# The m gates of the second half: a second turn by seven products, with moved row sums and other PSUM banks

## The chip, the cores and the metric

One core of one Trainium2 chip. The metric is the device time of one execution in microseconds (us), the median of several runs. The kernel before takes 2076.13 us (three runs, 2075.77 to 2076.33).

## The reference, cut to what matters

The kernel computes two blocks of a language model for 256 tokens of width 2048: a gated MLP mixer and then a block with attention, an mLSTM, a gated merge, an output projection and a feed-forward part. The change lies in the gated merge of the second block:

```python
g_a = jax.nn.sigmoid(z[..., OFF_GA:OFF_GM])
g_m = jax.nn.sigmoid(z[..., OFF_GM:D_IN])        # z = h @ w_in, h is 256 x 2048
merged = (g_a * jnp.einsum('bse,ed->bsd', a_out, w_proj_a[l])
          + g_m * jnp.einsum('bse,ed->bsd', m_out, w_proj_m[l]))
x = x + jnp.einsum('bsd,de->bse', merged, w_out[l])
```

The m gates are the product of h with 2048 columns of w_in. `gm0` computes their first 1024 columns, `gm1` the second 1024.

## The kernel before

**Number format.** Every matrix is split into a high and a low part, `w_hi` and `w_lo`, and a product is three matmuls (high by high, high by low, low by high). A weight chunk is 128 partitions by 1024: two blocks of 128 rows by 512 columns. It comes by DMA (SyncE's queue) into the four-slot ring `raw`; ScalarE copies it to `w_hi` (`high_of_chunk`, L1279), VectorE subtracts to get `w_lo` (`low_of_chunk`, L1778), TensorE uses both. `w_hi` and `w_lo` have four slots too: ScalarE's copy for item n waits until TensorE has ended item n - 4. In the loops over items, the turn for item n prepares item n + 4.

**Items.** The order of the work is written out by hand in `ITEMS`; every engine walks through it in its own loop. A phase such as gm0 covers two output tiles of 256 tokens by 512 columns (the halves, four PSUM banks of `g`, one for each half and token tile) and runs over 2048 rows of weights in four turns of 512 rows. A turn is done in one of two ways. *Plain*: four items C0 to C3, each a chunk of 12 matmuls. *By seven products* (Winograd's form of Strassen's scheme on 2 x 2 blocks): items named by their product, 1 to 7, each of 6 matmuls, 42 in place of 48. The seven products need sums of row blocks of the activations (`sums_hi`, `sums_lo`, made once for each turn and used again by the second half of the phase pair) and sums of weight blocks (`block_sums`, L1792: VectorE adds in place into the blocks that SyncE loaded, after the w_lo of products 1, 5 and 6 and of the item behind product 1). Products 1, 5, 6, 7 gather in banks of their own in `xs`, across all turns that go by products; products 2, 3, 4 go straight into `g`. After the last product 6, ScalarE copies product 1 out (`first_product`), VectorE combines the four (`own_products`, `last_of_own_products`), and `gate_m_result` (L2328) adds or subtracts them from the halves of `g`.

**How a seven is mixed with plain items.** While a product takes half of a plain item's matmuls, it needs a whole w_hi copy and a whole w_lo subtraction. So a seven is interleaved with the four items of a plain turn: `MIXED` is 1, C0, 5, 7, C1, 6, 3, C2, 4, 2, C3, and `MIXED_LATE` (used in gm1 and out2) is C0, 1, C1, 5, 7, C2, 6, 3, C3, 4, 2. gm0 runs turns 3 and 2 by products, mixed with plain turns 0 and 1. gm1 runs plain turn 0, then turn 3 by products mixed with plain turn 1, then plain turn 2.

**What lies around gm1.** The phases follow as gm0, pa0, pm0, gm1, pa1, pm1, out2; pa and pm are the projections of the two branches, 8 plain items each. At pm0's end VectorE makes the merged quarters: `merged_low(0)`, then `m_projected(0, 1)` (L2347 the gate product, L2349 the addition, which releases `merged_ready`). TensorE transposes the second quarter behind gm1's item 1 (`merged_turned(1)`, eight transposes into banks 0 and 1 of `xs`); ScalarE takes it with `merged_high(1)` in loop turn 1, VectorE with `merged_low(1)` (L2325, called at L2361) in loop turn 2, behind the w_lo and the block sum of that turn, and raises `merged_lo_ready` to 2. gm1's product 1 waits for that (L1197), since it writes bank 0. The merged values `g_hi` and `g_lo` take the memory of gm's row sums of turn 2, which is why gm1 before could use those of turn 3 alone.

Of the kernel before, what the change touches and what calls it, by code (L numbers as in the profile page):

```python
# [5 lines left out]
P = 128  # L6
# [52 lines left out]
for _name, _w in (("a_norm", KD), ("norm1", KD), ("norm2", KD), ("b_s", GROUPS),  # L59
# [33 lines left out]
    "down": (((3, None), (4, None), (8, None), (9, None), (5, 0), (6, 1), (7, 2), (10, None)),  # L93
             ((3, 0), (7, None), (4, 1), (5, 2), (8, 6), (9, None), (10, None))),
    "gm0": (((0, 3), (1, 2)),),
    "gm1": (((0, None), (1, 3), (2, None)),),
    "out2": (((0, None), (2, 1), (3, None)),) * 2,
}

# [50 lines left out]
for _name, _counts in PHASES:  # L150
    FIRST_ITEM[_name] = len(ITEMS)
    if _name == "ug":
        for _g in range(GROUPS):
            for _step in UG_ORDER if _g else UG_FIRST:
                if isinstance(_step, int):
                    ITEMS.append(Item("ug", _g, _step, UG_TURN, None, None))
                else:
                    _turn, _k = _step[0], int(_step[1][1])
                    ITEMS.append(Item("ug", _g, 0, _turn, _k // 2, 2 * _turn + _k % 2))
        continue  # L160
    if _name in MID_ORDER:
        for _g, _order in enumerate(MID_ORDER[_name]):
            for _step in _order:
                if isinstance(_step, int):
                    ITEMS.append(Item(_name, _g, _step, MID_TURN, None, None))
                else:
                    _turn, _k = _step[0], int(_step[1][1])
                    ITEMS.append(Item(_name, _g, 0, _turn, _k // 2, 2 * _turn + _k % 2))
        continue
    if _name not in WIDE_STEPS:  # L170
        ITEMS += [Item(_name, None, 0, None, None, _k) for _k in range(sum(_counts))]
        continue
    for _g, _steps in enumerate(WIDE_STEPS[_name]):
        for _turn, _by_products in _steps:
            for _what in (PLAIN if _by_products is None else MIXED_LATE if _name in ("gm1", "out2") else MIXED):
                if _what in PLAIN:
                    _k = int(_what[1])
                    ITEMS.append(Item(_name, _g, 0, _turn, _k // 2, 2 * _turn + _k % 2))
                else:
                    ITEMS.append(Item(_name, _g, _what, _by_products, None, None))  # L180
# [5 lines left out]
def in_ring(item):  # L186
# [39 lines left out]
             FIRST_ITEM["down"] + 13: ("down", B22), FIRST_ITEM["down"] + 14: ("down", B21),  # L226
             FIRST_ITEM["gm0"] - 4: ("gm0", B11), FIRST_ITEM["gm0"] - 3: ("gm0", B12),
             FIRST_ITEM["gm0"] - 2: ("gm0", B22), FIRST_ITEM["gm0"] - 1: ("gm0", B21),
             FIRST_ITEM["gm1"] - 2: ("gm1", B11), FIRST_ITEM["gm1"] - 1: ("gm1", B12),
             FIRST_ITEM["gm1"]: ("gm1", B22), FIRST_ITEM["gm1"] + 2: ("gm1", B21),  # L230
             FIRST_ITEM["out2"] - 2: ("out2", B11), FIRST_ITEM["out2"] - 1: ("out2", B12),
             FIRST_ITEM["out2"]: ("out2", B22), FIRST_ITEM["out2"] + 2: ("out2", B21)}

# [61 lines left out]

def own_banks(phase, g):

    if phase in ("ug", "vv"):
        return UG_OWN_BANK
    if phase == "side":  # L300
        return {0: TWO_BANKS, 1: FIRST_APART, 2: FIRST_APART}.get(g, ONE_BANK)
    return OWN_BANK
# [92 lines left out]
def build(nc, x, x_tokens, stream, w_s, params, gain_rows, final_rows, gate_w, identity, consts, out):  # L395
# [48 lines left out]
    class Mid:  # L444
# [3 lines left out]
        def __init__(self, sb, name, blocks, halves, sums):  # L448
# [2 lines left out]
            self.half = [sb(f"{name}_half{h}", "y", at * kib, [P, 2, COLS]) for h, at in enumerate(halves)]  # L451
            (self.p1, self.p7), (self.u_a, self.p5) = ((of[:, 0, :], of[:, 1, :]) for of in self.half)

    class Gated:


# [53 lines left out]
    for name, phase, groups, blocks, halves in (  # L510
# [43 lines left out]
    gm_wide = Wide(sb, "gm", [("mix", 0), ("mix", 4 * kib), ("y", 72 * kib), ("y", 76 * kib)],  # L554
                   [("y", 88 * kib), ("y", 64 * kib)], [("y", 92 * kib), ("y", 80 * kib)], ("y", 68 * kib),
                   ("y", 84 * kib), ("y", 32 * kib))
    out2_wide = Wide(sb, "o2", [("mix", 0), ("mix", 4 * kib), ("y", 48 * kib), ("y", 52 * kib)],
                     [("y", 56 * kib)], [("y", 60 * kib)], ("y", 72 * kib), ("y", 76 * kib), ("y", 0))
    g_hi = sb("g_hi", "y", 64 * kib, [P, KD, S], F32R)
# [13 lines left out]
    out1_wide = Wide(sb, "o", [("mix", 0), ("mix", 4 * kib), ("x", 12 * kib), ("x", 4 * kib)],  # L573
                     [("h", 8 * kib), ("h", 12 * kib)], [("h", 24 * kib), ("h", 28 * kib)], ("h", 0), ("h", 16 * kib),
                     ("y", 88 * kib))
    by_phase = {"vv": mid_sums, "v": v_wide, "out1": out1_wide, "gm0": gm_wide, "gm1": gm_wide, "out2": out2_wide, "down": down_wide}
    u_sum = sb("u_sum", "mix", 4 * kib, [P, 4, S])

    def wide(phase, g):
# [72 lines left out]
    with block:  # L652
# [71 lines left out]
        def _(pe):  # L724
# [149 lines left out]
            def opens_own(item):  # L874

                key = (item.phase, item.group, -item.product)
                new = key not in opened
                if new:
                    opened.add(key)
                    if item.phase in MID_ORDER:  # L880
                        opens_mid(item)
                    elif item.phase == "ug" and item.group and item.product in (1, 5):

                        pe.wait_ge(sem["sv_read"], item.group + 1)
                    elif item.phase == "ug" and item.group:

                        pe.wait_ge(sem["y_lo_ready"], item.group)
                    elif own_ahead(item.phase, item.group):
                        pe.wait_ge(sem["own_read"], own_ahead(item.phase, item.group))
                return new  # L890
# [293 lines left out]
            for p in range(2):  # L1184
                gm, pa, pm = f"gm{p}", f"pa{p}", f"pm{p}"
                for n in range(items_of(gm)):
                    at_item = FIRST_ITEM[gm] + n
                    item = ITEMS[at_item]
                    pe.wait_ge(lo_ready, at_item + 1)
                    if item.product:  # L1190
                        if item.product == 1 and p == 0:

                            pe.wait_ge(sem["m_done"], M_HEADS)
                            pe.wait_ge(sem["sums_lo_ready"], sums_ahead("gm0") + sum_slot("gm0", item.turn) + 1)
                        if item.product == 1 and p == 1:

                            pe.wait_ge(sem["merged_lo_ready"], 2)  # L1197
                        ins = wide_product(item, norm_mid.hi, norm_mid.lo, at_item % RING)
                    else:
                        ins = wide_chunk(item, norm_mid.hi, norm_mid.lo, at_item % RING)  # L1200
                    ins.then_inc(mm_done, 1)
                    if p and n == 1:
                        merged_turned(1)
                for n in range(8):
                    one(pa, n // 4, n % 4, tokens(pa, n // 4, am_hi[:, 0:8, :], am_lo[:, 0:8, :],
                                                  None if n >= 4 or p else "am_lo_ready"))
                for n in range(8):
                    one(pm, n // 4, n % 4, tokens(pm, n // 4, am_hi[:, 8:16, :], am_lo[:, 8:16, :],
                                                  None if n >= 4 or p else "am_lo_ready", 2))
                    if n == 6:  # L1210
                        merged_turned(2 * p)
# [63 lines left out]
        def _(act):  # L1275
# [405 lines left out]
            for p in range(2):  # L1681
                gm, pa, pm = f"gm{p}", f"pa{p}", f"pm{p}"
                for n in range(items_of(gm)):
                    split(gm, n)
                    if p and n == 1:
                        merged_high(1)
                    first_product(gm, FIRST_ITEM[gm] + n)
                for n in range(8):
                    split(pa, n)
                    if n in (1, 3):  # L1690
                        h = n // 2
                        act.wait_ge(group_read[h], group_of(gm, h)[2])
                        by_token(gate_m[h], gate_m[h], ACT.Tanh, scale_half).then_inc(sem["gate_m_ready"], 1)
                for n in range(8):
                    split(pm, n)
                    if n == 6:
                        merged_high(2 * p)
                    if p:
                        sums_high("out2", n - 8)
# [73 lines left out]
        def _(dve):  # L1773
# [119 lines left out]
            def own_products(phase, n):  # L1893
# [3 lines left out]
                for name, g in GROUPS_BY_PRODUCTS:  # L1897
                    if name != phase:
                        continue
                    after = n - product_item(phase, g, last_by_products(phase, g), 6)  # L1900
                    if after == 0:
                        dve.wait_ge(sem["p1_ready"], own_ahead(phase, g) + 1)
                        dve.wait_ge(mm_done, n + 1)
                        link(v.tensor_tensor(u_a[:], p1[:], XS[:, 2, :], ALU.subtract))
                    if after == 2:
                        link(v.tensor_tensor(u_b[:], XS[:, 3, :], u_a[:], ALU.add))
                    if after == 4:
                        link(v.tensor_tensor(u_a[:], XS[:, 1, :], u_a[:], ALU.add))

            def last_of_own_products(phase, n):  # L1910
                u_b, u_d = by_phase[phase].u_b, by_phase[phase].u_d
                for name, g in GROUPS_BY_PRODUCTS:
                    if name == phase and n - product_item(phase, g, last_by_products(phase, g), 6) == 5:
                        link(v.tensor_tensor(u_d[:], XS[:, 1, :], u_b[:], ALU.add))
                        dve.sem_inc(sem["own_read"], 1)

            def v_result(q):
# [433 lines left out]
            for p in range(2):  # L2351
# [14 lines left out]
                        a_projected(p, 0)  # L2366
                for n in range(8):
                    if n == 7:

                        merged_low(2 * p)  # L2370
                        m_projected(p, 1)
                    split(pm, n)
# [243 lines left out]
```

## Time and profile before

| | |
|---|---|
| median of three runs | 2076.13 us |
| the profiled execution | 2076.55 us |
| its span, first to last instruction | 2074.6 us |
| TensorE matmul busy | 2067.9 us (100%) |
| TensorE weight load busy | 1734.9 us (84%) |
| VectorE busy | 1640.2 us (79%) |
| ScalarE busy | 1163.1 us (56%) |
| granted TensorE clock, mean | 1.000 |

In the profile PE is TensorE (PEld its weight loads, which overlap), DVE is VectorE, ACT ScalarE, POOL GpSimd, SP SyncE. L906 is line 906 of the kernel. Matmuls overlap in their pipeline, so the duration of one is longer than the distance to the next. In a timeline row, the brackets behind an instruction tell how long its engine was idle before it and what ended that.

### The profile page before, as it was taken

The numbers are of one execution on the slowest core, as the hardware profiler recorded it, in microseconds if no ns is written. First come the engines' busy times: TensorE is split into PE (matmuls) and PEld (weight loads), VectorE is DVE, ScalarE is ACT, GpSimd is POOL, SyncE is SP. The second block draws the span as 40 slices with busy tenths as digits, with TensorE's granted clock in tenths as the row PEclk, the third lists the DMA queues.
The fourth block names the chain that finished last, engine by engine and source line by source line (L and its number), as shares of the span: only waits on it lengthen the run. The fifth ranks groups of instructions, "written<-read, shape, count | busy, mean of one in ns | idle before, by whom it ended". The sixth has DMA issues, their size and how long they took to land.

```text
span 2074.6 us, 25496 instructions
## 1 busy us (share of the span) xinstructions
PE 2067.9 (100%) x9916; PEld 1734.9 (84%) x9916; DVE 1640.2 (79%) x1846; ACT 1163.1 (56%) x1387; POOL 50.2 (2%) x53
## 2 busy tenths in 40 slices
PE   9999999999999999999999999999999999999999
PEld 7888888888888887878888888888888888888887
DVE  7988788887887876886788668867777777789986
ACT  6666555555556555655555455555555555555553
POOL 0000000000000000110000000000000000000000
PEclk9999999999999999999999999999999999999999
DMA  9667777787684667655475656455655555556663
GB/s 340 205 204 214 224 234 224 213 240 223 247 265 153 217 207 213 208 156 193 134 232 182 204 183 214 159 184 184 193 184 192 193 192 184 193 181 235 222 204 132
DMA packets 117720, 423.30 MB, mean 204 GB/s; under 512 B 13152, under 2 KB 13920, under 8 KB 117344
## 3 DMA queue, kind: packets, MB, share of 16 engines
q1 hardware_dynamic: 109440, 394.66, 57.1%
q0 software_dynamic: 5184, 18.88, 5.3%
q10 hardware_dynamic: 2976, 8.14, 1.1%
q8 instruction: 79, 1.29, 0.2%
q14 instruction: 41, 0.34, 0.1%
HBM read 419.52 MB, written 2.10 MB: 203 GB/s over the span
## 4 chain that ended last, share of the span: by engine, by line
PE 96%; DVE 3%; ACT 1%; DMA 1%; issue 0%; ACTq 0%; DVEq 0%
PE g L906 49%; PE xs L929 9%; PE xs L768 8%; PE g L768 8%; PE g L933 6%; PE g L739 4%; PE xs L774 4%; PE g L774 4%; PE xs L817 1%; DVE w_lo L1785 1%; PE xs L968 1%; PE xs L1101 0%; DMA raw<-in_stream 0%; ACT w_hi L1298 0%; DMA xf<-in_x 0%
## 5 line engine op out<-in xcount | busy, mean ns | idle before, releaser
L1785 DVE TENSOR_TENSOR w_lo<-raw,w_hi 128x1024 fp32r<-128x1024 f32 x631 | 765.2, 1222 | 314.1 <-ACT w_hi L1298 306.5
L1298 ACT ACTIVATE w_hi<-raw 128x1024 fp32r<-128x1024 f32 x631 | 661.8, 1057 | 522.4 <-PE g L906 224.3
L906 PE MATMUL g<-w_hi,in_both 128*128 128x512 f32 x1120 | 356.6, 390 | 1.8 <-DVE w_lo L1860 1.2
L906 PE MATMUL g<-w_hi,mid_both 128*128 128x512 f32 x992 | 320.2, 393 | 0.0
L906 PEld LDWEIGHTS g<-w_hi,in_both 128*128 128x128 f32 x1120 | 210.3, 188 | 47.1 <-DVE w_lo L1785 1.4
L906 PEld LDWEIGHTS g<-w_hi,mid_both 128*128 128x128 f32 x992 | 186.3, 188 | 38.5
L906 PE MATMUL g<-w_lo,in_both 128*128 128x512 f32 x560 | 217.9, 389 | 0.0
L906 PE MATMUL g<-w_lo,mid_both 128*128 128x512 f32 x496 | 193.1, 389 | 0.0
L768 PE MATMUL g<-mlp_both,w_hi 128*128 128x512 f32 x704 | 167.0, 391 | 0.0
L768 PE MATMUL xs<-mlp_both,w_hi 128*128 128x512 f32 x704 | 165.6, 390 | 0.0
L768 PEld LDWEIGHTS xs<-mlp_both,w_hi 128*128 128x128 f32 x704 | 130.7, 188 | 26.2
L768 PEld LDWEIGHTS g<-mlp_both,w_hi 128*128 128x128 f32 x704 | 130.4, 188 | 26.0
L906 PEld LDWEIGHTS g<-w_lo,in_both 128*128 128x128 f32 x560 | 105.2, 188 | 21.4
L906 PEld LDWEIGHTS g<-w_lo,mid_both 128*128 128x128 f32 x496 | 93.2, 188 | 18.7
L906 PE MATMUL g<-w_hi,f_hi 128*128 128x512 f32 x240 | 93.6, 390 | 0.1
L906 PE MATMUL g<-w_hi,f_lo 128*128 128x512 f32 x240 | 93.4, 389 | 0.0
L906 PE MATMUL g<-w_lo,f_hi 128*128 128x512 f32 x240 | 93.4, 389 | 0.0
L774 PEld LDWEIGHTS g<-mlp_both,w_lo 128*128 128x128 f32 x704 | 88.3, 191 | 2.3
L774 PE MATMUL g<-mlp_both,w_lo 128*128 128x256 f32 x704 | 89.0, 283 | 0.0
L774 PEld LDWEIGHTS xs<-mlp_both,w_lo 128*128 128x128 f32 x704 | 87.4, 192 | 1.7
L774 PE MATMUL xs<-mlp_both,w_lo 128*128 128x256 f32 x704 | 87.9, 283 | 0.0
L1298 ACT ACTIVATE w_hi<-d_block 128x1024 fp32r<-128x1024 f32 x49 | 52.0, 1062 | 56.5 <-PE g L906 39.4
(503 smaller groups left out, 3336.8 us busy)
## 6 DMA issues: line engine op xcount, KB each, us to landing
raw<-in_stream SPq DMA_DIRECT2D x631, 512.0 KB, 4.2
d_block<-in_stream SPq DMA_DIRECT2D x28, 512.0 KB, 4.6
o_block<-in_stream SPq DMA_DIRECT2D x24, 512.0 KB, 4.3
v_block<-in_stream SPq DMA_DIRECT2D x20, 512.0 KB, 4.3
ge_block<-in_stream POOLq DMA_DIRECT2D x15, 512.0 KB, 5.5
gm_block<-in_stream SPq DMA_DIRECT2D x12, 512.0 KB, 5.8
ge_block<-in_stream SPq DMA_DIRECT2D x10, 512.0 KB, 4.9
gl_block<-in_stream POOLq DMA_DIRECT2D x6, 512.0 KB, 5.7
```

The source lines that it names most:

```text
L739: ins = mm(G[buf][:, t, :], a[:, kt, at_t], w[:, slot, j * COLS:(j + 1) * COLS], start=(kt == 0 and n == 0), stop=(last and j == ROWS_PER_ ...
L768: return mm(UP[buf][:, b, :, :], w_hi[:, slot, j * COLS + b * P:j * COLS + (b + 1) * P], a_both[:, :, kt, :], start=(kt == 0), stop=last a ...
L774: ins = mm(UP[buf][:, b, 0, :], w_lo[:, slot, j * COLS + b * P:j * COLS + (b + 1) * P], a_both[:, 0, kt, :], start=False, stop=(last and j ...
L817: ins = turn(TR[:, b, t * P:(t + 1) * P], of[:, t, b * P:(b + 1) * P], ident[:])
L906: ins = mm(GG[:, bank, :], a[:, kt, t * P:(t + 1) * P], w[:, slot, half_chunk(j)], start=n == 0 and opens(item, bank), stop=ended and n == ...
L929: ins = mm(XS[:, own[p], :], a, w[:, slot, half_chunk(j)], start=first and opens_own(item), stop=last and j == 1 and n == 2, skip_group_ch ...
L933: ins = mm(GG[:, RESULT_OF[p], :], a, w[:, slot, half_chunk(j)], start=first and opens(item, RESULT_OF[p]), stop=False, skip_group_check=True)
L968: ins = mm(SV[:, t, :], w[:, t, :], a[:, t, :], start=(n == 0), stop=(n == 2))
L1298: activation(w_hi[:, n % RING, :], of[:], ACT.Copy).then_inc(hi_ready, 1)
L1785: v.tensor_tensor(w_lo[:, n % RING, :], of, w_hi[:, n % RING, :].bitcast(F32), ALU.subtract).then_inc(lo_ready, 1)
```

## The change

gm1 becomes what gm0 is, two turns by products: turn 3 mixed late with plain turn 0, then turn 2 mixed with plain turn 1 (22 items in place of 19). The row sums of turn 2 are copied by ScalarE, in loop turn 2 of pm0, from memory that the merged values are about to take to gate columns that are used up by then (`GatesLate`). Products 1 and 5 of gm1 use banks 2 and 3 and products 6 and 7 banks 0 and 1 (`UG_OWN_BANK`), and the wait for `merged_lo_ready` moves from product 1 to products 7 and 6. Block loads are asked for one item earlier. The loop turns in which `merged_turned(1)`, `merged_high(1)` and `merged_low(1)` are called stay as they are.

```diff
-    "gm1": (((0, None), (1, 3), (2, None)),),
+    "gm1": (((0, 3), (1, 2)),),
...
-            for _what in (PLAIN if _by_products is None else MIXED_LATE if _name in ("gm1", "out2") else MIXED):
+            _late = _name == "out2" or (_name, _turn) == ("gm1", 0)
+            for _what in (PLAIN if _by_products is None else MIXED_LATE if _late else MIXED):
...
-             FIRST_ITEM["gm1"] - 2: ("gm1", B11), FIRST_ITEM["gm1"] - 1: ("gm1", B12),
-             FIRST_ITEM["gm1"]: ("gm1", B22), FIRST_ITEM["gm1"] + 2: ("gm1", B21),
+             FIRST_ITEM["gm1"] - 3: ("gm1", B11), FIRST_ITEM["gm1"] - 2: ("gm1", B12),
+             FIRST_ITEM["gm1"] - 1: ("gm1", B22), FIRST_ITEM["gm1"] + 1: ("gm1", B21),
...
-    if phase in ("ug", "vv"):
+    if phase in ("ug", "vv", "gm1"):
         return UG_OWN_BANK
...
+    class GatesLate:
+        def __init__(self, sb, early, hi, lo):
+            self.moved_hi, self.moved_lo = sb("gm_moved_hi", *hi, [P, 4, 2, P], F32R), sb("gm_moved_lo", *lo, [P, 4, 2, P], F32R)
+            self.blocks = early.blocks
+            self.sums_hi, self.sums_lo = (early.sums_hi[0], self.moved_hi), (early.sums_lo[0], self.moved_lo)
+            self.p1, self.u_a, self.u_b, self.u_d = early.p1, early.u_a, early.u_b, early.u_d
...
+                    elif item.phase == "gm1":
+                        pe.wait_ge(sem["own_read"], own_ahead("gm1"))
+                        if item.product in (7, 6):
+                            pe.wait_ge(sem["merged_lo_ready"], 2)
...
-                        if item.product == 1 and p == 1:
-                            pe.wait_ge(sem["merged_lo_ready"], 2)
+                        if item.product == 1 and p == 1 and item.turn == SUM_TURNS["gm0"][1]:
+                            pe.wait_ge(sem["sums_moved"], 1)
...
                     split(pm, n)
+                    if n == 2 and p == 0:
+                        act.wait_ge(group_read[1], group_of("pa0", 1)[2])
+                        activation(gm_late.moved_hi[:], gm_wide.sums_hi[1][:].bitcast(F32), ACT.Copy)
+                        activation(gm_late.moved_lo[:], gm_wide.sums_lo[1][:].bitcast(F32), ACT.Copy).then_inc(
+                            sem["sums_moved"], 1)
                     if n == 6:
+                        if p == 0:
+                            act.wait_ge(sem["sums_moved"], 1)
                         merged_high(2 * p)
...
                     if n == 7:
+                        if p == 0:
+                            dve.wait_ge(sem["sums_moved"], 1)
                         merged_low(2 * p)
```

The remaining lines make `own_products` and `last_of_own_products` read the banks that `own_banks` names, and let gm1 use `gm_late`.

## Rows read from the trace of the kernel before

**Rows 1.** The page: span, and busy us, share and instructions of TensorE.

```profile
span 2074.6 us, 25496 instructions
...
PE 2067.9 (100%) x9916; PEld 1734.9 (84%) x9916; DVE 1640.2 (79%) x1846; ACT 1163.1 (56%) x1387; POOL 50.2 (2%) x53
```

**Rows 2.** Waits of TensorE: who waited for whom, us in total, times, longest.

```profile
PE xs L817 <- DVE col L2272: 0.5, 1, 0.5
```

**Rows 3.** Stages gm0 and gm1: length, busy us by engine, clock, DMA share, GB/s.

```profile
1088.91:1129.71 40.80, 40.80 (x181) 33.61 (x179) 36.83 (x34) 24.66 (x25) 0.00 (x0) 1.00 0.50 167
1174.54:1217.59 43.05, 43.05 (x195) 35.75 (x194) 34.79 (x33) 21.45 (x21) 0.00 (x0) 1.00 0.48 157
```

**Rows 4.** Timeline of TensorE in gm1: start us, us, line, operation; items' first matmuls.

```profile
1174.54 0.39 PE L906 MATMUL g<-w_hi,mid_both 128*128 128x512 f32 x1
...
1179.98 1.03 PE L817 MATMUL xs<-ident,gate_a 128*128 128x128 f32 x8
1180.77 0.48 PE L906 MATMUL g<-w_hi,mid_both 128*128 128x512 f32 x1
...
1189.03 0.39 PE L929 MATMUL xs<-w_hi,mid_both 128*128 128x512 f32 x1
...
1190.39 0.39 PE L906 MATMUL g<-w_hi,mid_both 128*128 128x512 f32 x1
...
1217.59 0.39 PE L739 MATMUL g<-w_hi,am_hi 128*128 128x512 f32 x1
```

**Rows 5.** Timeline of VectorE from the w_lo of gm1's item 1 on.

```profile
1170.35 1.22 DVE L1785 TENSOR_TENSOR w_lo<-raw,w_hi 128x1024 fp32r<-128x1024 f32 x1
...
1174.81 1.22 DVE L2347 SCALAR_TENSOR_TENSOR gate_m<-gate_m,g 128x1024 f32<-128x1024 f32 x1 [0.20 <-PE g L739]
1176.06 1.23 DVE L2349 TENSOR_TENSOR gate_a<-gate_a,gate_m 128x1024 f32<-128x1024 f32 x1
...
1181.33 1.22 DVE L1785 TENSOR_TENSOR w_lo<-gm_block,w_hi 128x1024 fp32r<-128x1024 f32 x1 [1.50 <-ACT w_hi L1298]
1182.69 1.23 DVE L1790 TENSOR_TENSOR gm_block<-gm_block,gm_block 128x1024 f32<-128x1024 f32 x1
1184.94 1.23 DVE L1785 TENSOR_TENSOR w_lo<-raw,w_hi 128x1024 fp32r<-128x1024 f32 x1 [1.03 <-ACT w_hi L1298]
1186.08 1.22 DVE L1790 TENSOR_TENSOR gm_block<-gm_block,gm_block 128x1024 f32<-128x1024 f32 x1
1187.22 1.22 DVE L2325 SCALAR_TENSOR_TENSOR g_lo<-xs,g_hi 128x1024 fp32r<-128x1024 f32 x1
```

**Rows 6.** Timeline of ScalarE: a row-sum copy (gm0), and w_hi copies in pm0 and gm1.

```profile
1076.54 1.04 ACT L1358 ACTIVATE gm_sums_hi<-gm_sums 128x1024 fp32r<-128x1024 f32 x1
...
1163.00 1.06 ACT L1298 ACTIVATE w_hi<-raw 128x1024 fp32r<-128x1024 f32 x1 [1.66 <-PE g L739]
...
1183.85 1.06 ACT L1298 ACTIVATE w_hi<-raw 128x1024 fp32r<-128x1024 f32 x1 [1.63 <-PE g L906]
...
1190.65 1.06 ACT L1298 ACTIVATE w_hi<-raw 128x1024 fp32r<-128x1024 f32 x1 [0.30 <-PE xs L929]
```

**Rows 7.** Timeline of VectorE and TensorE where gm0 ends and pa0 begins.

```profile
1128.62 1.28 DVE L2333 TENSOR_TENSOR gate_m<-g,gm_u 128x512 f32<-128x512 f32 x2
...
1129.48 0.39 PE L906 MATMUL g<-w_hi,mid_both 128*128 128x512 f32 x1
1129.96 0.50 PE L739 MATMUL g<-w_hi,am_hi 128*128 128x512 f32 x1
1130.30 0.39 PE L739 MATMUL g<-w_lo,am_hi 128*128 128x512 f32 x1
```

**Rows 8.** The tile gm_block: time of its 12 loads from issue to landing.

```profile
DMA to landing us min/median/max: 3.1/5.8/7.6
```

**Rows 9.** TensorE's first real matmul after the start's wait, and that stretch's clock.

```profile
7.81 0.47 PE L906 MATMUL g<-w_hi,in_both 128*128 128x512 f32 x1 [1.17 <-DVE w_lo L1860]
...
5.00:10.00 5.00, 3.83 (x25) 3.28 (x25) 3.41 (x7) 3.70 (x7) 0.00 (x0) 1.00 1.03 368
```

More of the change, by code:

```diff
@@ L556, in build @@
                    ("y", 84 * kib), ("y", 32 * kib))
+    gm_late = GatesLate(sb, gm_wide, ("y", 56 * kib), ("y", 60 * kib))
     out2_wide = Wide(sb, "o2", [("mix", 0), ("mix", 4 * kib), ("y", 48 * kib), ("y", 52 * kib)],
@@ L575, in build @@
                      ("y", 88 * kib))
-    by_phase = {"vv": mid_sums, "v": v_wide, "out1": out1_wide, "gm0": gm_wide, "gm1": gm_wide, "out2": out2_wide, "down": down_wide}
+    by_phase = {"vv": mid_sums, "v": v_wide, "out1": out1_wide, "gm0": gm_wide, "gm1": gm_late, "out2": out2_wide, "down": down_wide}
     u_sum = sb("u_sum", "mix", 4 * kib, [P, 4, S])
@@ L1899, in own_products @@
                         continue
+                    own = own_banks(phase, g)
                     after = n - product_item(phase, g, last_by_products(phase, g), 6)
@@ L1903, in own_products @@
                         dve.wait_ge(mm_done, n + 1)
-                        link(v.tensor_tensor(u_a[:], p1[:], XS[:, 2, :], ALU.subtract))
+                        link(v.tensor_tensor(u_a[:], p1[:], XS[:, own[6], :], ALU.subtract))
                     if after == 2:
-                        link(v.tensor_tensor(u_b[:], XS[:, 3, :], u_a[:], ALU.add))
+                        link(v.tensor_tensor(u_b[:], XS[:, own[7], :], u_a[:], ALU.add))
                     if after == 4:
-                        link(v.tensor_tensor(u_a[:], XS[:, 1, :], u_a[:], ALU.add))
+                        link(v.tensor_tensor(u_a[:], XS[:, own[5], :], u_a[:], ALU.add))
             def last_of_own_products(phase, n):
@@ L1913, in last_of_own_products @@
                     if name == phase and n - product_item(phase, g, last_by_products(phase, g), 6) == 5:
-                        link(v.tensor_tensor(u_d[:], XS[:, 1, :], u_b[:], ALU.add))
+                        link(v.tensor_tensor(u_d[:], XS[:, own_banks(phase, g)[5], :], u_b[:], ALU.add))
                         dve.sem_inc(sem["own_read"], 1)
```

## The prediction

> **What bounds the kernel now.** I read the page first: TensorE is busy for 2067.9 us of the span of 2074.6 us [rows 1]. Next I read who kept TensorE waiting: after the start the longest single wait is 0.5 us [rows 2]. So time can be won only by issuing fewer matmuls, and any wait that lands on TensorE is a full loss. The stage table shows the same inside the two m-gate stages: 40.80 of 40.80 us and 43.05 of 43.05 us, with VectorE at 36.83 and 34.79 us [rows 3]. VectorE is the engine to watch, because each item of seven products costs TensorE half of a plain item but VectorE a whole w_lo subtraction, and for four of the seven a block sum too.
>
> The busy column gives about 390 ns a matmul, but matmuls overlap, so I take start to start. Two plain items run from 1174.54 to 1179.98: 2.72 us each, 0.227 us a matmul. One product runs from 1189.03 to 1190.39: 1.36 us. The eight transposes with the plain item behind them run from 1179.98 to 1183.59: 3.61 us. The stage ends at 1217.59 [rows 4]. (1183.59 is the start of the w_hi copy at 1183.85 less 0.26, since the copy at 1190.65 started 0.26 after its own item's successor at 1190.39 [rows 4, 6].)
>
> I number the items of gm1 from 0. Before, items 0 to 3 are plain and product 1 is item 5. Afterwards the order is C0, 1, C1, 5, 7, C2, 6, 3, C3, 4, 2 and then 1, C0, 5, 7, C1, 6, 3, C2, 4, 2, C3.
>
> **Fewer matmuls.** Four plain items (48 matmuls) become seven products (42). Six matmuls fewer at 0.227 us: **-1.36 us**. The stage goes from 186 to 180 matmuls, as in gm0, whose 40.80 us are 180 x 0.227. This all lies on the path, because TensorE has no idle time there.
>
> **A wait that had cover and loses it.** The transposes of the second merged quarter write PSUM banks 0 and 1, which merged_high(1) and merged_low(1) must read before products may write them. Before, product 1 waits for this, five items into the stage: merged_low(1) ended at 1188.44 and product 1 started at 1189.03 [rows 4, 5], so the slack was 0.6 us. Afterwards products 1 and 5 use banks 2 and 3, and the wait stands before product 7, which is item 4. What the new bank order does not move is merged_low(1) itself: it stays in VectorE's order behind the w_lo of item 6, whose w_hi copy needs item 2 to have ended, since the ring has four slots. So I follow the chain.
>
> First the transposes. VectorE starts the w_lo of item 1 at 1170.35 as before [rows 5]. Items 1 and 2 now bring two block sums ahead of the merge. Spacings from the same rows: 1.36 from a w_lo to a sum that awaits it (1181.33 to 1182.69), 1.14 between other neighbours (1184.94, 1186.08, 1187.22), 1.25 from the gate product to its addition (1174.81 to 1176.06) [rows 5]. 1170.35 + 1.36 (sum) + 1.14 (w_lo 2) + 1.14 (sum) + 1.14 (merged_low(0)) + 1.14 (gate product) + 1.25 (addition) + 1.23 (its length) gives 1178.75. TensorE is ready for the transposes at 1174.54 + 2.72 + 1.36 = 1178.62. An end on VectorE reaches TensorE after 0.05 to 0.06 us (1128.62 + 1.28 to 1129.96 [rows 7]), so they start at 1178.80: **+0.18 us**. Before, the addition ended at 1177.29 and the transposes came at 1179.98.
>
> Then item 2 ends at 1178.80 + 3.61 = 1182.41 and product 5 at 1183.77. Meanwhile the w_hi copy of item 6 starts at 1182.41 + 0.26, its w_lo 1.09 later (1183.85 to 1184.94 [rows 5, 6]), the block sum 1.36 after that, merged_low(1) 1.14 after that and 1.22 long: 1187.48, on TensorE 1187.53. Product 7 wanted to start at 1183.77: **+3.76 us** of wait. The lower end takes the shorter spacing of 1.14 for the sum: 3.54. It cannot fall below that, as each link waits for the one before and the chain starts at the end of item 2 with only 1.36 us of TensorE work beside it. Behind the wait stand, on TensorE, all later matmuls; VectorE and ScalarE have work for items 7 and 8 only. The first matmul behind a wait costs 0.34 instead of 0.23 (1129.96 to 1130.30 [rows 7]): **+0.11 us**.
>
> **The end of gm1.** Its second half now runs in gm0's order. There the first gate subtraction ended at 1129.90, the last matmul started at 1129.48, so the next should have come at 1129.71 and came at 1129.96 [rows 7]. I take that pattern over: 0.25 + 0.11 = **+0.36 us**. In gm1 before there was none. Bounds: 0 and 0.5.
>
> **What is hidden.** The two copies of the row sums cost ScalarE 1.04 us each, in the first loop over pm0's items; each w_hi copy there comes after 1.66 us idle [rows 6]. They overrun by some 0.4 us, which the next copies' idle time absorbs; without that cover it would be 2.1 us. The new waits on sums_moved stand before merged_high(0) and merged_low(0), four loop turns later in both engines' order, and are long met there. Three more w_hi copies, three more w_lo subtractions and four more block sums make the stage's VectorE load like gm0's, which TensorE never waited on inside the stage [rows 3]. SyncE issues four block loads in place of four ring loads, equal in bytes; blocks asked for one item earlier go ahead of ring loads that are asked for four ring items in advance. The tightest is B22 of the second seven: asked for when the w_lo of product 4 is done, needed three items (1.36 + 1.36 + 2.72 us of TensorE work) later. Blocks landed in 3.1 to 7.6 us, median 5.8 [rows 8]. At the median product 7 of the second seven keeps about 0.4 us of slack, at the slowest it waits 1.3 us. I take 0, since TensorE lost nothing in gm0, which has the same in-place loads [rows 3].
>
> **The sum.** -1.36 + 0.18 + 3.76 + 0.11 + 0.36 = **+3.05 us**. The profiled execution took 2076.55 us with a span of 2074.6; it becomes 2079.6 with a span of 2077.7. The median of the three runs, 2076.13, lies 0.4 below that execution, and becomes **2079.2**. About 0.2%, or 4.15 us, is what a measurement of this kernel can tell from no change, so this is a small loss inside it. Its own bounds (3.54 for the wait, 0 to 0.5 at the end) with 0.3 us of scatter give 2078.3 to 2080.1.
>
> **Rivals.** *The clock falls.* A wait of 3.76 us is longer than any that TensorE has in this trace. What the rows show: after 1.17 us idle at the start, the matmuls ran at a granted clock of 1.00, the 2.4 GHz level [rows 9]. If the longer pause brings the 1.2 GHz level, a matmul takes 0.227 us more; for product 7 alone that is +1.4 us, for it and the plain item behind it +4.1: 2080.6 to 2083.3, slower than before by more than 0.2%. It decides from five matmuls at the lower level on. Against it: no row here shows that level at all. The Trainium skill, "TensorE: Matmul & The Clock Gate", "Why this matters for your kernels", asks for matmul bursts without idle gaps, since an idle gap takes the clock back to half rate; by it this wait may be dearer than its length, and no row of this trace shows such a gap either way.
>
> *The wait is hidden after all* (the merge is done earlier than I read, or product 7 is not what waits). Then -1.36 + 0.36 remains: 2075.1. For it speaks only that the wait was hidden before; against it the order of VectorE's program.
>
> *B22 lands late:* the forecast plus up to 1.3 us, 2080.5 at most.
>
> **Chances.** Forecast 0.72; clock 0.15; hidden 0.07; late block 0.05; else 0.01. The range leaves out the hidden wait and the upper half of the clock's case: 2076.8 to 2081.8. Slower by over 0.2% (above 2080.28): the clock's 0.15, most of the late block and the upper tail of the forecast: 0.21. Faster by over 0.2% has no case but the unknown: 0.01. Within: 0.78.
>
> **What would show it.** In the profile after: 180 matmuls in gm1, one wait of 3.5 to 3.8 us on TensorE before product 7 that ends with merged_low's VectorE row, 0.1 to 0.3 us before the transposes, 0.2 to 0.4 us before pa1, and a stage of some 46.1 us instead of 43.05. Wrong would be: no such wait, a matmul spacing of 0.45 us behind it, or a wait of VectorE on a block's DMA with TensorE waiting at the second product 7.

## The result and the profile after

The changed kernel takes 2081.36 us (median of 12 runs, 2079.47 to 2082.22) against 2076.19 us before (12 runs, 2075.77 to 2076.50). The ratio is 1.0024, with an interval of 1.0016 to 1.0031. So by the medians it is slower by 5.2 us. That lies inside the stated range, but 1.0 us beyond the 0.2% that the forecast of 2079.2 stayed within. The profiled execution took 2081.80 us.

The page of the kernel after, its span and its busy line, and under it the waits of TensorE (us in total, times, longest):

```profile
span 2079.8 us, 25505 instructions
...
PE 2070.1 (100%) x9910; PEld 1735.6 (83%) x9910; DVE 1647.8 (79%) x1853; ACT 1167.9 (56%) x1392; POOL 50.2 (2%) x53
```

```profile
PE xs L946 <- DVE g_lo L2351: 3.7, 1, 3.7
...
PE xs L829 <- DVE col L2298: 0.5, 1, 0.5
```

Before, 0.5 us was the longest wait after the start [rows 2]. Now one of 3.7 us stands above it: product 7 (L946) waits for merged_low(1) (L2351). Busy time says little here, since slow matmuls count as busy too. The timeline of TensorE in gm1 after, each row the first matmul of an item or a matmul that is named below:

```profile
1174.05 0.39 PE L923 MATMUL g<-w_hi,mid_both 128*128 128x512 f32 x1
...
1178.28 1.09 PE L829 MATMUL xs<-ident,gate_a 128*128 128x128 f32 x8
...
1181.98 0.39 PE L946 MATMUL xs<-w_hi,gm_sums_hi 128*128 128x512 f32 x1
...
1187.16 0.77 PE L946 MATMUL xs<-w_hi,gm_sums_hi 128*128 128x512 f32 x1 [3.67 <-DVE g_lo L2351]
1187.72 0.63 PE L946 MATMUL xs<-w_lo,gm_sums_hi 128*128 128x512 f32 x1
1188.15 0.63 PE L946 MATMUL xs<-w_hi,gm_sums_lo 128*128 128x512 f32 x1
...
1192.78 0.39 PE L923 MATMUL g<-w_lo,mid_both 128*128 128x512 f32 x1
1193.01 0.62 PE L923 MATMUL g<-w_hi,mid_both 128*128 128x512 f32 x2
...
1193.92 0.39 PE L946 MATMUL xs<-w_hi,gm_sums_hi 128*128 128x512 f32 x1
...
1222.26 0.39 PE L923 MATMUL g<-w_hi,mid_both 128*128 128x512 f32 x1
1222.73 0.50 PE L751 MATMUL g<-w_hi,am_hi 128*128 128x512 f32 x1
```

Read it against [rows 4]. The stage now runs from 1174.05 to 1222.73, 48.68 us instead of 43.05. Item by item:

- C0 and product 1 would end at 1174.05 + 4.08 = 1178.13; the transposes start at 1178.28: +0.15.
- Transposes and C1 take 3.70 us (1178.28 to 1181.98) instead of 3.61: +0.09.
- Product 5 would end at 1183.34; product 7 starts at 1187.16: **+3.82**. (The profile counts 3.67, from the end of the last matmul, which it shows 0.39 us long, while the next could have started 0.23 us after its start.)
- Product 7 and C2 take 6.76 us (1187.16 to 1193.92) instead of 4.08: **+2.68**. From 1187.72 to 1188.15 a matmul takes 0.43 us, at the end (1192.78 to 1193.01) 0.23 us again.
- The end: 1222.26 + 0.23 = 1222.49, the next matmul at 1222.73: +0.24, and 0.11 more on that matmul.

With -1.36 for six matmuls this is 5.62 us for the stage (and the 0.11 behind it). The stage starts 0.49 us earlier than before in these two executions. Of that, 0.48 us is already there where gm0 begins (1088.43 against 1088.91), and so far ahead of the change; this is why the spans differ by 5.2 us and not by 5.7.

The stretches by time, after (length, then busy us of PE, PEld, DVE, ACT, POOL, then the granted clock as a share of 2.4 GHz, DMA share, GB/s):

```profile
1183.00:1187.00 4.00, 0.50 (x3) 0.07 (x1) 3.57 (x4) 1.35 (x2) 0.00 (x0) 0.86 0.65 240
1187.00:1190.00 3.00, 2.84 (x7) 2.31 (x8) 1.15 (x2) 0.00 (x0) 0.00 (x0) 0.50 0.23 86
1190.00:1193.00 3.00, 3.00 (x9) 2.38 (x8) 1.22 (x1) 1.06 (x1) 0.00 (x0) 0.55 0.25 94
1193.00:1196.00 3.00, 3.00 (x15) 2.47 (x14) 0.73 (x1) 1.52 (x2) 0.00 (x0) 1.00 0.52 175
```

Behind the pause the clock stands at 0.50, the 1.2 GHz level, and comes back before 1193. In [rows 3] it was 1.00 in the whole stage. The first row shows that it fell while TensorE still stood: with two levels, a mean of 0.86 over 4 us is some 1.1 us at the lower one (an estimate from the row), so the fall came about 1185.9, some 2.4 us into the pause. VectorE's chain that makes the pause, after:

```profile
1177.00 1.23 DVE L2375 TENSOR_TENSOR gate_a<-gate_a,gate_m 128x1024 f32<-128x1024 f32 x1
...
1183.33 1.23 DVE L1810 TENSOR_TENSOR w_lo<-gm_block,w_hi 128x1024 fp32r<-128x1024 f32 x1 [0.44 <-ACT w_hi L1315]
1184.66 1.22 DVE L1815 TENSOR_TENSOR gm_block<-gm_block,gm_block 128x1024 f32<-128x1024 f32 x1
1185.80 1.22 DVE L2351 SCALAR_TENSOR_TENSOR g_lo<-xs,g_hi 128x1024 fp32r<-128x1024 f32 x1
```

This is the chain of the prediction link by link [rows 5]: w_lo of item 6, block sum 1.33 us later, merged_low(1) 1.14 us later, done at 1187.02. TensorE starts 0.14 us after that; the prediction had 0.05 to 0.06.

### The profile page after: what moved, and what is told of

It is laid out like the page before. It is cut to its first block, busy times and chain, and to the rows that moved or that the text cites. A ratio compares the mean times of both kernels' runs of the same rounds, so it can differ in the third digit from the quotient of the medians.

```text
span 2079.8 us, 25505 instructions
## 1 busy us (share of the span) xinstructions
PE 2070.1 (100%) x9910; PEld 1735.6 (83%) x9910; DVE 1647.8 (79%) x1853; ACT 1167.9 (56%) x1392; POOL 50.2 (2%) x53
## 4 chain that ended last, share of the span: by engine, by line
PE 96%; DVE 3%; ACT 1%; issue 0%; DMA 0%; ACTq 0%; DVEq 0%
PE g L923 49%; PE xs L946 9%; PE xs L780 8%; PE g L780 8%; PE g L950 6%; PE g L751 4%; PE xs L786 4%; PE g L786 4%; DVE w_lo L1810 1%; PE xs L829 1%; PE xs L985 1%; ACT w_hi L1315 1%; PE xs L1118 0%; DMA xf<-in_x 0%; PE xs L1115 0%
## 5 line engine op out<-in xcount | busy, mean ns | idle before, releaser
L923 PE MATMUL g<-w_hi,mid_both 128*128 128x512 f32 x960 | 311.7, 394 | 0.0
L923 PEld LDWEIGHTS g<-w_hi,mid_both 128*128 128x128 f32 x960 | 181.0, 188 | 37.5
L923 PE MATMUL g<-w_lo,mid_both 128*128 128x512 f32 x480 | 187.4, 390 | 0.0
```

What stands on the lines that cost most here:

```text
L923: ins = mm(GG[:, bank, :], a[:, kt, t * P:(t + 1) * P], w[:, slot, half_chunk(j)], start=n == 0 and opens(item, bank), stop=ended and n == ...
```

## The experiments

The clock of each execution is known as its mean over the span, so each kernel's executions can be told apart by whether it fell below 1.000. "At 1.000" is the median of those in which it did not. The mean has three decimals: a stretch at the lower level of less than about 2 us (an estimate: 0.0005 of some 2075 us, twice) would still read 1.000. The pause is that of the profiled execution.

| kernel | median us | runs | pause before the waiting product, us | runs below clock 1.000 | at 1.000 | below |
|---|---|---|---|---|---|---|
| before (run beside e1 to e4) | 2076.16 | 29 | none | 0 | 2076.16 | |
| after | 2081.36 | 12 | 3.67 | 10 | 2079.68 | 2081.48 |
| e1_early_merge | 2075.36 | 11 | none | 0 | 2075.36 | |
| e2_plain_first | 2076.83 | 11 | 0.95 | 0 | 2076.83 | |
| e3_shorter_wait | 2079.55 | 11 | 2.34 | 6 | 2078.39 | 2079.74 |
| e4_wait_in_before | 2081.74 | 7 | 3.65 | 6 | 2080.16 | 2081.75 |
| before (run beside e5 to e7) | 2076.33 | 27 | none | 0 | 2076.33 | |
| e5_early_both | 2074.84 | 11 | none | 0 | 2074.84 | |
| e6_before_gm0_end | 2075.99 | 11 | none | 0 | 2075.99 | |
| e7_filled_wait | 2079.57 | 11 | 0.27 | 0 | 2079.57 | |

Theory A: the loss is TensorE's pause at product 7 and the lower clock that the pause brings. Theory B: the loss is spread over the denser sevens, their block sums, the copies and the loads.

**e1_early_merge: the pause taken away.**

```diff
+                    if p and n == 1:
+                        merged_low(1)
                     split(gm, n)
-                    if p and n == 2:
-                        merged_low(1)
```

> The changed kernel with one edit: VectorE takes the low part of the second merged quarter (merged_low(1)) one loop turn earlier, ahead of the w_lo of item 5 instead of behind the w_lo and the block sum of item 6. Theory A (the loss is the wait of TensorE at product 7, 3.7 us, plus the lower clock that follows it): both go, and what stays is -1.36 for the matmuls, +0.2 at the transposes, +0.36 at the end of gm1: 2075.4 us, clock 1.000. Theory B (the loss is spread: the denser sevens, their extra block sums, the copies and the block loads): 2079 to 2081 us.

Measured: 2075.36 us, all 11 runs between 2075.18 and 2075.87; ratio 0.9996 (0.9987 to 1.0004). VectorE's and then TensorE's timeline of this run:

```profile
1180.56 1.22 DVE L1810 TENSOR_TENSOR w_lo<-gm_block,w_hi 128x1024 fp32r<-128x1024 f32 x1
1181.70 1.22 DVE L2351 SCALAR_TENSOR_TENSOR g_lo<-xs,g_hi 128x1024 fp32r<-128x1024 f32 x1
1182.83 1.21 DVE L1810 TENSOR_TENSOR w_lo<-raw,w_hi 128x1024 fp32r<-128x1024 f32 x1
```

```profile
1183.12 0.39 PE L946 MATMUL xs<-w_hi,gm_sums_lo 128*128 128x512 f32 x1
1183.35 0.39 PE L946 MATMUL xs<-w_hi,gm_sums_hi 128*128 128x512 f32 x1
```

merged_low(1) ends at 1182.92, and product 7 starts at 1183.35, 0.23 us behind product 5's last matmul: no pause. Everything else of the change is in place, and 6.0 us are gone. Theory B falls. Against the kernel before, the 0.8 us gained by the medians are not clear of that interval.

**e2_plain_first: other work put beside the chain.**

```diff
+MIXED_C2 = ("C0", 1, "C1", 5, "C2", 7, 6, 3, "C3", 4, 2)
...
-            _late = _name == "out2" or (_name, _turn) == ("gm1", 0)
-            for _what in (PLAIN if _by_products is None else MIXED_LATE if _late else MIXED):
+            _late = _name == "out2"
+            _order = MIXED_C2 if (_name, _turn) == ("gm1", 0) else MIXED_LATE if _late else MIXED
+            for _what in (PLAIN if _by_products is None else _order):
```

> The changed kernel with plain item C2 put ahead of product 7 in gm1's first seven; the merge stays late. Theory A: 2.72 us of work now lie beside the chain that ends with merged_low(1), so the wait before product 7 shrinks from 3.7 to 1.0 us and the clock stays at 2.4 GHz: -1.36 + 0.2 + 1.0 + 0.11 + 0.36 = +0.3, 2076.5 us. Rival on the clock (any wait of a microsecond or more brings the 1.2 GHz level): 2077.5 to 2079 us. Theory B: 2079 to 2081 us.

Measured: 2076.83 us. TensorE's last matmul of C2 and first of product 7 in this run:

```profile
1185.98 0.39 PE L925 MATMUL g<-w_hi,mid_both 128*128 128x512 f32 x1
1187.32 0.47 PE L948 MATMUL xs<-w_hi,gm_sums_hi 128*128 128x512 f32 x1 [0.95 <-DVE g_lo L2353]
```

The pause of 0.95 us was expected at 1.0. The clock was 1.000 in all 11 runs, and 1.00 behind the pause in the profiled one, so the rival on the clock falls. The time is 0.3 us above the expected one. From start to start the wait is 1.11 us (1185.98 + 0.23 to 1187.32), which is 0.1 us of that; where the rest lies is not shown.

**e3_shorter_wait: a pause in between.**

```diff
-                    split(gm, n)
                     if p and n == 2:
+                        low_of_chunk(at_item + RING)
                         merged_low(1)
+                        block_sums(at_item + RING)
+                    else:
+                        split(gm, n)
```

> The changed kernel with merged_low(1) between the w_lo and the block sum of item 6, so that it ends 1.2 us earlier. Theory A: a wait of 2.5 us before product 7 instead of 3.7. With the clock at 2.4 GHz that gives -1.36 + 0.2 + 2.5 + 0.11 + 0.36 = +1.8, 2078.0 us; if this wait brings the lower level as the one of 3.7 us did, 2079 to 2080.4 us. Theory B: 2079 to 2081 us with no change against the changed kernel.

Measured: both of the times that were named. Five of 11 runs kept clock 1.000 and lie at 2078.05 to 2078.71, six fell to 0.999 and lie at 2079.55 to 2080.20. The profiled execution is one of the first kind; TensorE's timeline:

```profile
1186.11 0.47 PE L946 MATMUL xs<-w_hi,gm_sums_hi 128*128 128x512 f32 x1 [2.34 <-DVE g_lo L2351]
1186.41 0.39 PE L946 MATMUL xs<-w_lo,gm_sums_hi 128*128 128x512 f32 x1
1186.64 0.40 PE L946 MATMUL xs<-w_hi,gm_sums_lo 128*128 128x512 f32 x1
```

After the pause the second and third matmul are 0.23 us apart, full speed. So a pause of 2.34 us brings the lower level in some executions and not in others; the six are told by their mean clock and time, since none of them was profiled.

**e4_wait_in_before: the pause alone, without the change.**

```diff
                     split(gm, n)
-                    if p and n == 2:
+                    if p and n == 4:
                         merged_low(1)
```

> The kernel before with one edit: merged_low(1) two loop turns later, so that product 1 of gm1, which waits for it, stands still for some 3.7 us; no other order, bank or copy is changed. Theory A with the clock following from the wait alone: +3.75 + 0.11 for the wait, and +1 to +2.5 for matmuls at the 1.2 GHz level in most executions: 2081 to 2082.5 us, median near 2081.9, clock 0.998 to 0.999. Rival (the fall of the clock belongs to the new order, with its products of half length): the wait alone, 2080.1 us, clock 1.000.

Measured: 2081.74 us; the one run at clock 1.000 took 2080.16, the other six 2081.49 to 2083.20. VectorE's merged_low(1), TensorE's timeline, and the clock at the end of the pause and behind it (columns as above):

```profile
1191.28 1.22 DVE L2325 SCALAR_TENSOR_TENSOR g_lo<-xs,g_hi 128x1024 fp32r<-128x1024 f32 x1
...
1192.60 0.76 PE L929 MATMUL xs<-w_hi,mid_both 128*128 128x512 f32 x1 [3.65 <-issue]
1193.16 0.63 PE L929 MATMUL xs<-w_lo,mid_both 128*128 128x512 f32 x1
1193.59 1.05 PE L929 MATMUL xs<-w_hi,mid_both 128*128 128x512 f32 x2
...
1192.00:1194.00 2.00, 1.40 (x3) 1.16 (x4) 0.49 (x1) 0.00 (x0) 0.00 (x0) 0.62 0.04 8
1194.00:1196.00 2.00, 2.00 (x6) 1.60 (x5) 0.00 (x0) 0.41 (x1) 0.00 (x0) 0.53 0.00 0
```

The profile names no releaser here ("issue"), but product 1 starts 0.10 us after merged_low(1) ends at 1192.50. A pause of the same length in the old order, with the old banks and no copies, costs about as much (5.6 us) and brings the same clock. The rival falls: the new order is not needed for it. By the same estimate as above, the clock fell here about 1192.5, some 3.5 us into the pause that began at 1188.95, against 2.4 us in the kernel after. So the fall does not come at a fixed distance from the pause's start, and that a pause of 2.34 us is hit in some executions only fits this. What sets the moment is not shown.

**e7_filled_wait: the pause kept, but filled.** Behind product 5 of the first seven, TensorE repeats one matmul 15 times.

```diff
+                if item.phase == "gm1" and p == 5 and not last:
+                    for _ in range(15):
+                        ins = mm(XS[:, own[p], :], hi, w_hi[:, slot, half_chunk(1)], start=False, stop=False, skip_group_check=True)
                 return ins
```

> The changed kernel with 15 more matmuls behind product 5 of gm1's first seven (they add product 5's last term again, so the gates of the second half are not the reference's): TensorE works for 3.4 of the 3.7 us that it waited. The end of the merge, and so the start of product 7, stays where it is. If the lower clock comes from TensorE standing still: clock 1.000 in every execution and 2079.4 us, where the changed kernel's executions at clock 1.000 lie, -2 us against its median. Rival (the lower clock comes from something else at this place, such as the traffic of VectorE and the DMAs, or the denser sevens): 2081.4 us and clock 0.998 to 0.999 as in the changed kernel.

Measured: 2079.57 us, clock 1.000 in all 11 runs. TensorE's timeline, and the two stretches in which the kernel after stood at 0.86 and 0.50:

```profile
1183.50 3.56 PE L954 MATMUL xs<-w_hi,gm_sums_hi 128*128 128x512 f32 x15
1187.33 0.47 PE L946 MATMUL xs<-w_hi,gm_sums_hi 128*128 128x512 f32 x1 [0.27 <-DVE g_lo L2354]
1187.64 0.39 PE L946 MATMUL xs<-w_lo,gm_sums_hi 128*128 128x512 f32 x1
...
1183.00:1187.00 4.00, 4.00 (x18) 3.01 (x17) 3.48 (x4) 0.46 (x1) 0.00 (x0) 1.00 0.83 255
1187.00:1190.00 3.00, 2.73 (x13) 2.23 (x13) 1.41 (x2) 2.01 (x2) 0.00 (x0) 1.00 0.02 5
```

Product 7 starts as late as in the kernel after, and 15 matmuls of no use make the kernel 1.8 us faster. The filling also holds back item 7's w_hi copy and w_lo, but in the filled stretch VectorE (3.48 us) and the DMAs (0.83) are about as busy as, or busier than, in the kernel after (3.57 us and 0.65), so their traffic is not what lowers the clock. With e4 this shows the cause: the clock falls because TensorE stands still.

**e5_early_both and e6_before_gm0_end: the gap at the stage's end.** e5 is e1 with the edit below for gm0 and gm1, e6 the kernel before with it for gm0 alone.

```diff
-                        if at_item == half_end(gm, 0, h):
+                        if at_item == half_end(gm, 0, h) - (h == 0):
                             gate_m_result(gm, h)
```

> The kernel with the early merge (first run of the study, 2075.36 us) and one more edit: in gm0 and gm1 VectorE makes the first gate half (gate_m_result(0)) one loop turn earlier, ahead of the w_lo of item 23 instead of behind it. Theory A: the 0.36 us between the end of each m-gate stage and its first projection matmul goes, twice: 2075.36 - 0.72 = 2074.6 us, below the kernel before. Rival (the gap at the stage's end has another cause, such as the first matmul of another phase): no change, 2075.4 us.

> The kernel before with the same edit of gate_m_result(0) in gm0 alone, so that what the change is worth can be read against a kernel before that has this too. Theory A: 0.36 us less, 2075.8 us. Rival: no change, 2076.2 us.

Measured: e5 2074.84 us (ratio 0.9993, 0.9984 to 1.0001), e6 2075.99 us (ratio 0.9998, 0.9989 to 1.0007). Against their own runs of the kernel before that is -1.49 and -0.34 us; e1 stood at -0.80 against its own. So the edit brings 0.34 us for gm0 alone and 0.69 for both, against 0.36 and 0.72 expected. VectorE's and TensorE's timeline of e5 at the end of gm1:

```profile
1213.73 1.29 DVE L2359 TENSOR_TENSOR gate_m<-g,gm_u 128x512 f32<-128x512 f32 x2
1214.94 1.22 DVE L1810 TENSOR_TENSOR w_lo<-raw,w_hi 128x1024 fp32r<-128x1024 f32 x1
```

```profile
1215.73 0.39 PE L923 MATMUL g<-w_hi,mid_both 128*128 128x512 f32 x1
1215.96 0.39 PE L751 MATMUL g<-w_hi,am_hi 128*128 128x512 f32 x1
```

The gate half now ends at 1215.02, before TensorE's last matmul of the stage, and the next phase follows 0.23 us later, where [rows 7] had 0.48. e5 is the best version: its slowest run (2075.50) is below the fastest of the kernel before beside it (2075.91). The interval of its ratio, which allows for more than the scatter of these runs, still touches 1, as that of e6 does; that the gap itself is gone the timelines show. Between e5 and e6, which share gm0's edit, the change is worth -1.15 us, near the -1.36 of its six matmuls plus 0.24 at the transposes.

## Why the prediction was right, and where it was not

**The matmuls.** 180 for 186 at 0.227 us, -1.36 us: right, as e5 against e6 shows once the waits are gone.

**The wait at product 7.** Expected 3.76 us, measured 3.82 (3.67 by the profile's own count). The chain came link by link, but for the step from VectorE to TensorE (0.14 for 0.05 us). This part carried the sign of the forecast, and e1 shows that it is the loss: moving one VectorE instruction brings back 6.0 us.

**The transposes and the end.** 0.18 expected, 0.15 measured, with 0.09 more in the transposes and C1 that no term had; 0.25 + 0.11 expected at the end, 0.24 + 0.11 measured, confirmed by e5 and e6.

**What was hidden.** The two copies, in ScalarE's timeline after:

```profile
1160.75 1.04 ACT L1716 ACTIVATE gm_moved_hi<-gm_sums_hi 128x1024 fp32r<-128x1024 f32 x1
1161.70 1.05 ACT L1717 ACTIVATE gm_moved_lo<-gm_sums_lo 128x1024 fp32r<-128x1024 f32 x1
1162.65 1.04 ACT L1315 ACTIVATE w_hi<-raw 128x1024 fp32r<-128x1024 f32 x1
1165.23 1.06 ACT L1315 ACTIVATE w_hi<-raw 128x1024 fp32r<-128x1024 f32 x1 [1.53 <-PE g L751]
```

They use up the idle time of 1.66 us [rows 6]; the next w_hi copy follows at once, and the one behind it has 1.53 us to spare again. No late block: besides what is listed above, TensorE waited for nothing in the stage. The price of B22 was rightly taken as 0, though neither its 0.4 nor its 1.3 us follows from the 5.44 us of the three items that the prediction names. The prediction's upper bound of 2080.1 does not come out either: 2079.2 + 0.14 at the end + 0.3 is 2079.6.

**The clock.** Here the step that failed is a chance: 0.72 for a clock that stays up behind the wait, 0.15 for one that falls. The sum of +3.05 us is the time of an execution in which the clock stays at 2.4 GHz: the two such executions of the kernel after took 2079.47 and 2079.89, +3.3 and +3.7. But ten of 12 were of the rival's kind, at 2080.70 to 2082.22. Its price was right: +1.4 to +4.1 expected, +1.8 measured between the medians of the two kinds, +2.57 in the profiled execution, where the 5.6 us from 1187.16 to 1192.78 are some 13 of the 18 matmuls at 0.43 us. Its time, 2080.6 to 2083.3, holds the measured 2081.36. The prediction's own sign of being wrong, a spacing of 0.45 us behind the wait, came (0.43). What misled was the argument against it, that no row shows the lower level: no row of the trace before shows a long pause either, so the trace could not speak for or against, and the longest pause in it, of 1.17 us at the start [rows 9], is about as long as that of e2, which does no harm. The rule of the Trainium skill, "TensorE: Matmul & The Clock Gate", "Why this matters for your kernels", that a long idle gap between matmul bursts takes the clock back to half rate, was cited and then weighed too lightly. These traces agree with it: the clock was 0.50 behind the pause of 3.67 us. They also go beyond it: a gap of 2.34 us, shorter than those the page warns of, did so in six of 11 executions.

So the forecast named the likelier of the two cases wrongly, and the result lies 2.2 us above it. It is inside the range because that had been drawn across part of the rival's case. That it ended 0.4 us inside the upper end is luck in part: how many executions fall, and how long each stays slow, was in no term.

## What to carry to other kernels

When a wait is moved on an engine that never idles, follow the chain that ends it, instruction by instruction in the other engine's program order; half as much TensorE work per item means half the cover for an instruction that stays in its old loop turn. Do not price a TensorE pause as its length alone: here pauses of 2.34 to 3.67 us cost, in the executions whose clock fell, some 1.3 to 1.8 us more by the medians. And look first for the one instruction to move: with the merge one loop turn earlier the same change stands at 0.8 us less than before, by the medians, where it had lost 5.2.

## What the runs showed of the hardware

The lower clock is not certain behind a pause: it showed in none of 11 runs at 0.95 us, six of 11 at 2.34, six of seven at 3.65, ten of 12 at 3.67. These runs tell the first number from the others; whether the share still rises from 2.34 us on, they are too few to tell. The fall came some 2.4 us into one profiled pause and 3.5 us into another, while TensorE stood. The lower level nearly halves the matmul's speed (0.43 for 0.23 us) for a stretch that is not the same in every run: from the first matmul behind the pause it lasted some 5.5 us in the kernel after and 3.3 us in e4 (estimates from the clock rows), and the extra time ran from 1.0 to 2.5 us over the executions of the kernel after. With 15 matmuls whose result nobody needs in the pause, it showed in none of 11 executions.
